# Three of the four heads' outputs transposed by a DRAM round trip and VectorE 32 by 32 turns instead of by TensorE

## The reference

```python
o = jnp.einsum('bchls,bcshv->bclhv', scores, v)
...
o = o + jnp.einsum('bclhd,bchdv->bclhv', q_fwd, s_prev)
o = rmsnorm(o.reshape(bsz, seq, GLA_HEADS, GLA_DV), norm_g.reshape(GLA_HEADS, GLA_DV))
o = o.reshape(bsz, seq, vd) * jax.nn.silu(r.astype(f32))
return (o @ w_out).astype(h.dtype)
```

## Time and profile before

| | |
|---|---|
| Median of 3 runs | 2189.22 us (2187.75 to 2190.8) |
| Profiled execution | 2190.93 us, its span 2189.2 us |
| PE busy | 2150.1 us, 98% of the span |
| GpSimd busy | 1628.4 us, 74% |
| DVE busy | 1385.2 us, 63% |
| ACT busy | 823.7 us, 38% |
| Granted clock of PE over the span | 0.996 |

### The profile page before, as it was taken

One profiled execution on the slowest core, in us unless ns is written; L12 is line 12 of the kernel. 1 busy time (PEld: TensorE's weight loads), 2 busy tenths in 40 slices (PEclk: granted clock), 3 DMA queues, 4 the chain that ended last, 5 costly groups with the idle time before them and its releaser, 6 DMA issues.

```text
span 2189.2 us, 27841 instructions
## 1 busy us (share of the span) xinstructions
PE 2150.1 (98%) x9922; PEld 1778.4 (81%) x9922; DVE 1385.2 (63%) x1800; ACT 823.7 (38%) x1461; POOL 1628.4 (74%) x1294
## 2 busy tenths in 40 slices
PE   8999999999999999999999998999999999999997
PEld 6888888878887888788888877888888888888886
DVE  6445544554565554278787855766667577978796
ACT  4233433343344332344444433444434422142223
POOL 7646675667566756788898868888888886878784
PEclk9999999999999999999999999999999999999999
DMA  5222354335433645745545458343434588659773
GB/s 178 87 68 81 121 192 127 115 121 187 131 120 116 203 154 206 255 169 202 178 180 186 164 209 338 144 173 126 174 134 173 197 322 317 266 218 358 272 309 124
DMA packets 225545, 404.75 MB, mean 185 GB/s; under 512 B 17184, under 2 KB 156448, under 8 KB 216448
## 3 DMA queue, kind: packets, MB, share of 16 engines
q1 hardware_dynamic: 190448, 360.44, 46.1%
q10 hardware_dynamic: 34960, 42.54, 5.8%
HBM read 273.94 MB, written 128.97 MB: 184 GB/s over the span
## 4 chain that ended last, share of the span: by engine, by line
PE 61%; DVE 3%; POOL 2%; issue 1%; DMA 1%; ACT 0%; SPq 0%; ACTq 0%; POOLq 0%; DVEq 0%
PE ps L735 20%; PE ps L737 20%; PE ps L736 20%; DVE acc L2019 1%; POOL ring_lo L663 1%; DMA x_op<-xop 1%; POOL ring_hi L660 0%; POOL w_op L672 0%; DVE xs L1547 0%; DMA raw<-in_gla_w_out 0%; PE ps L870 0%; DVE acc L1986 0%; SPq L473 0%; DVE p_sum L2019 0%; DMA raw<-in_gla_w_in 0%
## 5 line engine op out<-in xcount | busy, mean ns | idle before, releaser
L672 POOL TENSOR_TENSOR w_op<-w_raw,w_op 128x512 fp32r<-128x512 f32 x330 | 482.4, 1473 | 112.5 <-ACT w_op L1085 109.3
L735 PE MATMUL ps<-x_op,w_op 128*128 128x512 f32 x1232 | 481.3, 391 | 10.4 <-issue 3.3
L736 PE MATMUL ps<-x_op,w_op 128*128 128x512 f32 x1232 | 480.4, 390 | 0.0
L737 PE MATMUL ps<-x_op,w_op 128*128 128x512 f32 x1232 | 480.3, 390 | 0.0
L660 POOL TENSOR_SCALAR ring_hi<-raw 128x512 fp32r<-128x512 f32 x256 | 179.0, 699 | 289.6 <-issue 180.8
L663 POOL TENSOR_TENSOR ring_lo<-raw,ring_hi 128x512 fp32r<-128x512 f32 x256 | 349.8, 1367 | 21.3
L1085 ACT ACTIVATE w_op<-w_raw 128x512 fp32r<-128x512 f32 x330 | 202.7, 626 | 375.9 <-POOL w_raw L690 148.8
L735 PEld LDWEIGHTS ps<-x_op,w_op 128*128 128x128 f32 x1232 | 231.9, 188 | 60.4 <-issue 9.8
L737 PEld LDWEIGHTS ps<-x_op,w_op 128*128 128x128 f32 x1232 | 231.9, 188 | 48.5
L736 PEld LDWEIGHTS ps<-x_op,w_op 128*128 128x128 f32 x1232 | 232.0, 188 | 48.0
L735 PE MATMUL ps<-w_op,hid 128*128 128x512 f32 x616 | 240.7, 391 | 1.7 <-DVE acc L2019 0.8
(11 more groups left out here) (206 smaller groups left out, 3995.2 us busy)
## 6 DMA issues: line engine op xcount, KB each, us to landing
hop<-stage SPq DMA_DIRECT2D x154, 512.0 KB, 2.8
hid<-hop SPq DMA_DIRECT2D x70, 1024.0 KB, 9.4
raw<-in_gla_w_in SPq DMA_DIRECT2D x192, 256.0 KB, 3.3
w_raw<-in_ffn_w_gu SPq DMA_DIRECT2D x176, 256.0 KB, 4.0
w_raw<-in_ffn_w_down SPq DMA_DIRECT2D x88, 256.0 KB, 4.5
xop<-x_stage ACTq DMA_DIRECT2D x42, 512.0 KB, 3.4
x_op<-xop SPq DMA_DIRECT2D x36, 512.0 KB, 8.5
raw<-in_gla_w_out SPq DMA_DIRECT2D x64, 256.0 KB, 3.0
```

The lines of the kernel that those rows point to most:

```text
L672: pool.tensor_tensor(shaped(q, tile[:, 1, :]), source(q, i), shaped(q, tile[:, 0, :]).bitcast(F32), ALU.subtract).then_inc(op_ready[i], 1)
L735: pe.matmul(out, l_hi, r_hi, start=first, stop=False, skip_group_check=more)
L736: pe.matmul(out, l_hi, r_lo, start=False, stop=False, skip_group_check=more)
L737: return pe.matmul(out, l_lo, r_hi, start=False, stop=last, skip_group_check=more)
```

## The change

- `turn_o(n)` on PE goes for heads 0 to 2 of each block. PE now waits for `og_done` of the head before where it waited for `oT_lo_done` in `make_scores`.
- Instead SP stores `og` of such a head to DRAM (`store_og`, 512 KB) and loads it back into the same place in SBUF in another order (`load_og`, four loads of 32 partitions, in runs of 64 columns, 256 bytes). Partition 32i + s, block m then holds token 32m + s, columns 64i to 64i + 63.
- DVE turns this in 32 by 32 squares, every second column (`turn_o_blocks`: two `transpose` of 128 by 512), into `oT`, in the next head behind its last state step and ahead of `under_o`. (`oT` lies in the place of `oT_lo`.)
- ACT takes the high part in one piece of 128 by 1024 before the next head's squares; DVE the low part in one piece of 128 by 1024, from SBUF instead of PSUM, behind `under_o` and ahead of the variance.
- Head 3 of a block is still transposed by PE, now with every second column of `og`. The rows of `w_out` are loaded in the order that goes with this.

```diff
-    o_w = w_out[0].rearrange("(k p) n -> p k n", p=P)
+    o_w = w_out[0].rearrange("(h p j) n -> h j p n", p=P, j=2)
...
+            def store_og(b, hd):
+                sp.wait_ge(og_done, NT * (b * H + hd + 1))
+                sp.dma_start(og_kept[:, :].rearrange("(t p) c -> p t c", p=P), og[:, :, :]).then_inc(og_stored, 16)
+
+            def load_og(b, hd):
+                sp.wait_ge(og_stored, 16 * (b * (H - 1) + hd + 1))
+                by_32 = og_kept[:, :].rearrange("(m s) (i c) -> i s m c", s=32, i=4)
+                for i in range(4):
+                    sp.dma_start(og_by_32[32 * i:32 * i + 32, :, :], by_32[i]).then_inc(og_loaded, 16)
...
                     i = b * ROUNDS + 3 * hd
+                    if hd >= 2:
+                        store_og(b, hd - 2)
                     columns(i, 0, q_w, hd * DK)
                     columns(i, 1, k_w, hd * DK)
+                    def og_back():
+                        if hd >= 2:
+                            load_og(b, hd - 2)
...
+                    load_vr(i + 1, hd, 0, og_back)
...
+                store_og(b, H - 2)
                 i = b * ROUNDS + ROUND_OUT
                 for n in range(4):
                     load_out(i + n // 2, n)
+                    if n == 0:
+                        load_og(b, H - 2)
...
-                if n > 0:
-                    pe.wait_ge(oT_lo_done, 2 * n)
-                if n > 0 and n % H == 0:
+                if n % H > 0:
+                    pe.wait_ge(og_done, NT * n)
+                elif n > 0:
+                    pe.wait_ge(oT_lo_done, (H + 1) * (n // H))
...
-                        ins = pe.transpose(ps[:, 6 + j, t * P:(t + 1) * P], og[:, t, j * P:(j + 1) * P], ident[:, :])
+                        ins = pe.transpose(ps[:, 6 + j, t * P:(t + 1) * P], og[:, t, j::2], ident[:, :])
...
                     vr_unit(i + 4, 0, 2)
-                    turn_o(n)
                     vr_unit(i + 4, 0, 3)
...
                 act.activation(r_gate[:, :, :], ps[:, 2:6, DV:], ACT.Silu).then_inc(r_silu, 1)
                 under_o()
+                if hd > 0:
+                    turned_o_hi(b, hd - 1)
...
                 if hd == H - 1:
                     gate_r(n)
+                if hd > 0:
+                    turn_o_blocks(b, hd - 1)
                 under_o()
+                if hd > 0:
+                    turned_o_lo(b, hd - 1)
                 variance_of(DV, SQUARES[b, f"head{hd}"] + NT, slice(0, NT))
...
+            def turn_o_blocks(b, hd):
+                dve.wait_ge(og_loaded, 16 * 4 * ((H - 1) * b + hd + 1))
+                for j in range(2):
+                    ins = dve.transpose(oT[:, 2 * hd + j, :].rearrange("p (m s) -> p m s", s=32),
+                                        og_by_32[:, :, j::2])
+                ins.then_inc(oT_blocks, 1)
```

More of the change, by code:

```diff
@@ L410, in columns @@
                                   w[:, 4 * u:4 * u + 4, start:start + P]) for u in range(2)])
-            def rows(i, p, w, k, start):
-                load_pair(i, p, [(raw[:, p, u, :], w[:, k + u, start:start + UNIT]) for u in range(2)])
             def load_quad(q):
@@ L488, in wait_operands, with load_vr @@
                         sp.wait_ge(xop_stored[n], late_stored(n, 2 * len(LATE)))
-            def load_vr(i, hd, n, next_x=None):
+            def load_vr(i, hd, n, between):
                 for p in range(2):
@@ L494, in load_vr @@
                                      (raw[:, p, :, DV:], r_w[:, k:k + 2, hd * DV:(hd + 1) * DV])])
-                    if p == 0 and next_x is not None:
-                        wait_operands(next_x - 1)
-                        load_x(next_x)
+                    if p == 0:
+                        between()
             def load_out(i, n):
-                half, k2 = divmod(n, KV // 2)
-                rows(i, n % 2, o_w, 2 * k2, half * HALF)
+                half, hd = divmod(n, H)
+                load_pair(i, n % 2, [(raw[:, n % 2, j, :], o_w[hd, j, :, half * HALF:half * HALF + UNIT])
+                                     for j in range(2)])
+            def store_og(b, hd):
[6 more added lines that the diff above has]
+                    sp.dma_start(og_by_32[32 * i:32 * i + 32, :, :], by_32[i]).then_inc(og_loaded, 16)
             for b in range(NB):
@@ L505, in _, with next_x @@
                     i = b * ROUNDS + 3 * hd
+                    if hd >= 2:
+                        store_og(b, hd - 2)
                     columns(i, 0, q_w, hd * DK)
                     columns(i, 1, k_w, hd * DK)
-                    load_vr(i + 1, hd, 0)
+                    def og_back():
+                        if hd >= 2:
+                            load_og(b, hd - 2)
+                    def next_x():
+                        if hd == H - 1 and 0 < b < NB - 1:
+                            wait_operands(b)
+                            load_x(b + 1)
+                    load_vr(i + 1, hd, 0, og_back)
                     if hd == 1 and b > 0:
@@ L512, in _ @@
                         load_h(b)
-                    load_vr(i + 2, hd, 1, b + 1 if hd == H - 1 and 0 < b < NB - 1 else None)
+                    load_vr(i + 2, hd, 1, next_x)
                     if hd in (1, 2) and b == NB - 1:
@@ L693, in _ @@
                 if q == 0:
[L694 removed]
+                    pool.wait_ge(oT_done, 2 * NB)
                 if q != 2:
@@ L958, in _ @@
                         turn_o(n)
+                        pe.wait_ge(oT_lo_done, (H + 1) * b + H - 1)
                     if m == 6:
-                        pe.wait_ge(oT_lo_done, 2 * n + 2)
+                        pe.wait_ge(oT_lo_done, (H + 1) * (b + 1))
                     if m == KV and more:
@@ L1226, in turned_o_hi, with turned_last_hi @@
             def turned_o_hi(b, hd):
-                n = b * H + hd
+                act.wait_ge(oT_blocks, (H - 1) * b + hd + 1)
+                parts = slice(2 * hd, 2 * hd + 2)
+                split_hi(oT_hi[:, parts, :], oT[:, parts, :]).then_inc(oT_hi_done, 1)
+            def turned_last_hi(b):
                 for j in range(2):
-                    act.wait_ge(oT_done, 2 * n + j + 1)
+                    act.wait_ge(oT_done, 2 * b + j + 1)
                     act.nop(nofuse=True)
-                    split_hi(oT_hi[:, 2 * hd + j, :], ps[:, 6 + j, :]).then_inc(oT_hi_done, 1)
+                    split_hi(oT_hi[:, KV - 2 + j, :], ps[:, 6 + j, :]).then_inc(oT_hi_done, 1)
             def square_next(b):
@@ L1738, in head, with turned_last_lo @@
                                              op1=ALU.mult).then_inc(og_done, 1)
+            def turn_o_blocks(b, hd):
[4 more added lines that the diff above has]
+                ins.then_inc(oT_blocks, 1)
             def turned_o_lo(b, hd):
-                n = b * H + hd
+                dve.wait_ge(oT_hi_done, (H + 1) * b + hd + 1)
+                parts = slice(2 * hd, 2 * hd + 2)
+                split_lo(oT_lo[:, parts, :], oT[:, parts, :], oT_hi[:, parts, :]).then_inc(oT_lo_done, 1)
+            def turned_last_lo(b):
                 for j in range(2):
-                    dve.wait_ge(oT_hi_done, 2 * n + j + 1)
-                    split_lo(oT_lo[:, 2 * hd + j, :], ps[:, 6 + j, :], oT_hi[:, 2 * hd + j, :]).then_inc(oT_lo_done, 1)
+                    dve.wait_ge(oT_hi_done, (H + 1) * b + H + j)
+                    split_lo(oT_lo[:, KV - 2 + j, :], ps[:, 6 + j, :], oT_hi[:, KV - 2 + j, :]).then_inc(oT_lo_done, 1)
             dve.memset(scores[:, :, :], 0.0)
@@ L1857, in _ @@
                     turned_lo(b + 1, 1, 4)
-                turned_o_lo(b, H - 1)
+                turned_last_lo(b)
                 if more:
```

12 lines of the change are left out of this document (7 added, 5 removed).

## The result

The changed kernel takes 2193.17 us in the median of 20 runs, the kernel before 2189.61 in as many; the ratio is 1.0017, 95% interval 1.0011 to 1.0023. So it is 3.6 us slower (2.4 to 5.0), where 2.1 us less was forecast. Against the 0.2% that I took for the limit of a measurement this is no change; against its own interval it is a small loss, and the sign of the forecast was wrong.

The account below looks back on a forecast made before the run. TensorE, busy 875.1 of 890 us in the mixer, was taken as the bound. 10.6 freed - 8.1 - 0.4 in stops = 2.1 us less, 2187.1 against a median of 2189.2; range 2180 to 2195.

Parts of the forecast that it names:

- the 0.2% that I took for the limit of a measurement: Whole kernel: a measurement can tell about 0.2%, 4.4 us, from no change.
- the sign of the forecast: Whole kernel: faster, by 2.1 us.
- What goes, 10.6 us.: TensorE, heads 0 to 2: 12 removed turns at 0.88 us each free 10.6 us, the largest possible gain.
- No idle time stands before them, so all of it is TensorE's own time.: At the removed turns on TensorE: with no idle time before them, the whole 10.6 us is TensorE's own time.
- That is little room, but enough, and both sides move with TensorE.: Ring unit 3 behind a removed turn: GpSimd needs about 2.1 us, TensorE has 2.7 us of work in between.
- What follows on every engine starts from TensorE's turns and moves with them, so I count nothing further: After the second token turn in head 3 of blocks 0 to 2: all engines move with TensorE's turns, nothing further counted.
- The loads on SP behind the round trip, "I cost it at nothing": SP queue: second half of the round's weights waits behind the `og` loads, cost nothing; loads take 4 to 8 us, no wait.
- Turns 0.68, ACT's high part 1.1, low part 1.2.: Lengths of added work: each VectorE turn 0.68 us, ACT's high part 1.1, DVE's low part 1.2.
- Heads 1 and 2 covered.: At `make_scores` in heads 1 and 2 of each block: 1.3 us or more of room left, gain of 0.88 stays.
- Head 3, 2.7 us in each of three blocks.: Second token turn, blocks 0 to 2: `xT_lo` comes late through DVE's longer chain and GpSimd; stops of 2.7 us, 8.1 together.
- Block 3, 0.4; the strided turn, nothing.: Block 3: a 0.4 us stop at TensorE's turn of `og`; strided reading of `og` in head 3's turns costs nothing.
- the forecast's own pattern: Head 3's chain: DVE and GpSimd instructions lengthen each other where they meet; variance took 0.59, one root step 0.89 us.

Follow-up runs that it names:

- Experiment 1: The kernel before without the TensorE turns of heads 0 to 2 and nothing in their place (output not the reference's): 2181.38 us, ratio 0.9965.
- experiment 9: The kernel before without those turns: with GpSimd's sum and the token loads moved, 2193.26 us; with the sum alone moved, 2178.55 us.
- experiment 2: The changed kernel without the store to DRAM and loads back; DVE turns `og` as it lies (output not the reference's): 2188.91 us, ratio 1.0003.
- experiment 3: The kernel before with the same store and loads added, for which DVE waits and which nobody uses: 2189.56 us, ratio 0.9999.
- experiment 8: The changed kernel with late high and low parts in head 3 and GpSimd's sum moved, without the DRAM trip (output not the reference's): 2180.69 us, ratio 0.9959.
- Experiment 4: The changed kernel; in head 3 of blocks 0 to 2 ACT's high part behind the root, DVE's low part behind the first `xT_lo` pair: 2184.84 us.
- experiment 6: The changed kernel with head 2 turned by TensorE as before, only heads 0 and 1 through DRAM: 2187.39 us; with GpSimd's sum moved, 2181.89 us.
- experiment 7: The changed kernel with late parts in head 3 and GpSimd's sum moved, plus token loads behind round 27's second half of weights: 2193.14 us, ratio 1.0017.

## Why the prediction was wrong, step by step

- *What goes, 10.6 us.* Right: 0.89 a turn and 10.7 in all by the alignment.
- *"No idle time stands before them, so all of it is TensorE's own time."* True at the place itself, wrong as a statement on the end. A later place had no room: in head 1 of block 1 GpSimd was ready 0.05 us ahead of TensorE, so what TensorE gained on it before that place was given back there. Experiment 1 shows it with the turns alone, experiment 9 that the place of GpSimd's work decides and not a pace over the whole mixer.
- *"That is little room, but enough, and both sides move with TensorE."* For the unit behind a removed turn it held: no stop there. As a statement on the ring it is the step that failed, together with *"What follows on every engine starts from TensorE's turns and moves with them, so I count nothing further"*. I read the ring at the end of head 3, where GpSimd waits for TensorE, and took it for all heads. In head 1 GpSimd works in one row, on weights that come by DMA and on sums, and moves with TensorE only in part (2.9 of 4.6 us in experiment 1). Costed at nothing, the ring's stops in head 1 and the slow matmuls behind the first took 4.8 us.
- *The loads on SP behind the round trip, "I cost it at nothing".* Half right. The loads themselves were in time, 4.0 us to landing where I took 4 to 8, and no row has DVE waiting for them. (The factor of two in the estimate beside the Trainium skill, "DMA: Bandwidth & Descriptors", was my own and not the page's.) But the time that GpSimd waits for raw weights rose from 10.5 to 18.6 us in the mixer (11.3 in experiment 2, without the trip). The wait of 2.27 us in the chain of head 1 doesn't come of the trip: it is 2.05 without it. Without the trip experiment 2 has 0.14% less than the changed kernel, some 3 us; experiment 3 has nothing and experiment 8 about 1 us in the medians. In the mixer of the profiled executions it is 2.0, 2.0 and 3.7 us. What the traffic costs, between 0 and 4 us, stays open, and so does where.
- *Turns 0.68, ACT's high part 1.1, low part 1.2.* 0.688, 1.062 and 1.226. The Trainium skill, "VectorE: DVE Perf Modes", The three transpose paths, would by an estimate, four times its 311 ns, have given 1.24 for 512 columns; the measured 0.688 is little more than half of that. That would fit a fixed part paid once for the whole instruction, but no run has a turn of another width to show it.
- *Heads 1 and 2 covered.* Right for what was costed: in head 1 of block 1 `scale_qk` ends at 349.4 and TensorE comes at 351.15.
- *Head 3, 2.7 us in each of three blocks.* The mechanism and the stepping came out: the low part lengthened by GpSimd, `xT_lo` last. The size is 2.0 each, 6.0 instead of 8.1, as the root met one GpSimd instruction for 0.9 us. Experiment 4 removes exactly these stops.
- *"What follows on every engine starts from TensorE's turns and moves with them, so I count nothing further."* Wrong for head 3 of blocks 1 and 2 too, 3.3 us at `v_lo` and `state_in`. In block 2 both sides of the change bring it about alone: experiments 1 and 9, with nothing added, have it, and so has experiment 3, with nothing removed; with head 2's turn kept (experiment 6) it is gone. The `newton` steps in the root of the tokens meet GpSimd's splits there, and their longer time is the size of the stop (experiment 7). That a small step of DVE waits until GpSimd's instruction is over, the rows show; it was the forecast's own pattern, used at one place and not looked for at the others. Why it hits in one run and misses in the next is a matter of some tenths of a us between engines, and I can't predict it.
- *Block 3, 0.4; the strided turn, nothing.* No stop at head 3's turn in block 3, and a strided turn costs 0.07 us more (865.61 to 866.47 against 861.63 to 862.42).

By the prediction's own sum, with what was measured: 10.7 - 6.0 for the stop that I knew would have been 4.7 us faster. The stops costed at nothing, 4.8 + 3.3 + 1.1 less 1.1 that came back, make 3.4 us slower of it. The one stop that was costed came out 2.1 us smaller than forecast, which hides part of this.

## What to carry to other kernels

When time is taken from the engine that bounds, follow that engine forward and note at every handoff how long its supplier was ready before it; where that is near zero, what was freed upstream is given back there, so the largest gain is what the tightest supplier allows, wherever it is. Clear that supplier first: one sum of GpSimd moved took 2 us off the kernel before in the medians (0.2 to 3.9; 0.4 in its mixer's trace) and 2.8 to 5.5 us off those with fewer turns on TensorE. A queue that serves several engines is ordered by who stops first: moving token loads behind weights cost 11 us; ACT waits for the tokens, and in its order stands in front of TensorE's operand.

## What the runs showed of the hardware

- A stop can cost more than its length. After TensorE had stood for 2.58 us (changed kernel), 2.23 (experiment 2), 2.32 (changed kernel with the sum moved) and 4.90 (experiment 7) the granted clock fell to between 0.50 and 0.65 in the next 2 to 3 us; after 1.86 and 1.71 it stayed at 1.00. The two stops of 2.13 in experiment 6 went both ways: 1.00 behind that of block 1, 0.50 behind that of block 2. So the length alone doesn't tell. The slow matmuls cost another 1.6 to 1.7 us behind the stops of 2.58, 2.32 and 2.13.
- A 32 by 32 turn on VectorE of 128 x 512 fp32 takes 0.688 us, as much as a two-input instruction of that width. All 24 read every second column; none with unit stride was run.
- Reading every second column of `og` for a TensorE transpose makes its weight load 209 ns instead of 138 to 143, and the turn of eight only 0.07 us longer.
- A DRAM to SBUF load of 128 KB in runs of 256 bytes lands after 4.0 us (median of 48) among other loads; 256 KB of weights beside it land after 3.4.
- VectorE's instructions of 0.16 us took up to 1.22 in the changed kernel, always beside a GpSimd instruction, its two-input `ring_lo` or its one-input `ring_hi`. The Trainium skill, "SBUF — State Buffer", Who interferes with whom, says that the two engines share a port pair which one locks at a time, and that an instruction with one SBUF input outside the perf modes needs only VectorE's own. The rows of `newton`, with two inputs, agree. The `variance`, with one input, is lengthened as well, from 0.17 to as much as 1.22; no run shows in which mode it ran.
- Whether GpSimd lengthens a VectorE transpose, no run shows: the 24 transposes of the changed kernel stayed at 668 to 707 ns, but GpSimd was idle during every one of them, and so it was in the other runs that have them.
